# Neighbourhood attention over 160 keys a tile, with the tokens laid out by grid columns

## The reference

```python
h = rmsnorm(x, norm1_g);  proj = h @ w_in + b_in          # width 4352
qa, ka, va, qb, kb, vb, ga, gb = split(proj)
oa = neighborhood_attention(qa, ka, va, rpb)  # 8 heads of 64; a query sees all 4 rows and the 16 grid
                                              # columns nearest to its own (clamped), bias by 2-D offset
ob = sliding_window_gqa(rope(qb), rope(kb), vb, sinks)    # 8 heads, 2 KV heads, |i - j| <= 128
x = x + (sigmoid(ga) * (oa @ w_up_a) + sigmoid(gb) * (ob @ w_up_b)) @ w_out
x = x + moe(rmsnorm(x, norm2_g))              # top 4 of 32 experts: 1024 -> 2 x 1024 -> 1024
return rmsnorm(x, final_g)
```

## Time and profile before

| | |
|---|---|
| median of 3 runs | 1115.62 us |
| lowest and highest | 1115.27 and 1117.86 us |
| the profiled execution | 1115.38 us |
| its span (first to last instruction) | 1113.1 us |
| mean granted clock of TensorE, share of full speed | 0.994 |
| PE busy | 1074.6 us, 97% of the span |
| DVE, ACT, POOL busy | 303.9, 110.8, 43.2 us |
| HBM read | 434.26 MB, 391 GB/s over the span |
| chain that ended last | PE 67%, DMA 26%, SP's queue 4% |

### The profile page before, as it was taken

The page is one execution under the profiler, slowest core; times in us unless marked ns, Lnnn a source line. Parts: engine busy times, 40 slices in busy tenths (PEclk is TensorE's granted clock), DMA queues, the critical chain, the costliest instruction groups (busy, mean ns, idle before and its releaser), DMA issues.

```text
span 1113.1 us, 13392 instructions
## 1 busy us (share of the span) xinstructions
PE 1074.6 (97%) x5309; PEld 479.3 (43%) x5309; DVE 303.9 (27%) x659; ACT 110.8 (10%) x243; POOL 43.2 (4%) x44
## 2 busy tenths in 40 slices
PE   9999999999999999999999999999999999999996
PEld 8888888633333333333333333333332333333332
DVE  4356644222222222122222222222221112222213
ACT  1142520200000000000000000000000000000001
POOL 1106500000000000000000000000000000000000
PEclk9999999999999999999999999999999999999999
DMA  9963379599999999999999999999999999999996
GB/s 360 410 238 121 114 261 389 216 425 427 427 429 429 429 429 427 429 427 427 430 427 429 428 428 429 427 429 427 430 427 430 427 430 427 429 428 429 429 425 277
DMA packets 35641, 435.69 MB, mean 391 GB/s; under 512 B 4384, under 2 KB 4896, under 8 KB 6848
## 3 DMA queue, kind: packets, MB, share of 16 engines
q1 hardware_dynamic: 34608, 434.38, 92.9%
q10 hardware_dynamic: 1008, 0.95, 0.3%
HBM read 434.26 MB, written 1.05 MB: 391 GB/s over the span
## 4 chain that ended last, share of the span: by engine, by line
PE 67%; DMA 26%; SPq 4%; DVE 1%; ACT 1%; issue 0%; POOLq 0%; POOL 0%; DVEq 0%
PE bank L893 26%; DMA ring<-in_w 25%; PE bank L959 13%; PE bank L606 5%; SPq L371 4%; PE bank L854 4%; PE bank L799 4%; PE bank L806 3%; PE bank L708 3%; PE bank L690 2%; PE bank L550 2%; PE bank L602 1%; PE bank L782 1%; PE bank L654 1%; PE bank L627 1%; DMA ring<-in_w_in 1%
## 5 line engine op out<-in xcount | busy, mean ns | idle before, releaser
L893 PE MATMUL bank<-ring,work 128*64 128x512 f32 x2048 | 452.9, 595 | 24.8 <-DMA ring<-in_w 24.8
L893 PEld LDWEIGHTS bank<-ring,work 128*64 128x64 f32 x2048 | 147.1, 137 | 309.6 <-issue 274.9
L959 PE MATMUL bank<-ring,work 128*64 128x512 f32 x1024 | 232.5, 596 | 1.0 <-DVE work L1377 0.6
L1367 DVE TENSOR_SCALAR work<-bank 128x512 f32<-128x512 f32 x32 | 22.1, 692 | 398.3 <-PE bank L893 398.3
L959 PEld LDWEIGHTS bank<-ring,work 128*64 128x64 f32 x1024 | 70.4, 136 | 134.6 <-issue 114.6
L1551 ACT ACTIVATE work<-work 128x512 f32<-128x512 f32 x32 | 20.1, 629 | 696.8 <-DVE work L1367 696.8
L799 PE MATMUL bank<-x2n,work 128*64 128x512 f32 x256 | 68.5, 616 | 0.0
L854 PE MATMUL bank<-work 64*128 64x512 f32 x256 | 63.9, 617 | 0.9 <-DVE work L1345 0.9
L1291 DVE TENSOR_TENSOR work<-bank,vec 128x256 f32<-128x256 f32 (+1 forms) x64 | 24.1, 418 | 144.0 <-PE bank L806 144.0
L806 PEld LDWEIGHTS bank<-cst,work 128*128 128x128 f32 x320 | 33.8, 141 | 54.9 <-DVE work L1374 27.4
L606 PE MATMUL bank<-ring 128*128 128x256 f32 x240 | 54.2, 382 | 0.0
(11 more groups left out here) (203 smaller groups left out, 570.2 us busy)
## 6 DMA issues: line engine op xcount, KB each, us to landing
ring<-in_w SPq DMA_DIRECT2D x184, 2048.0 KB, 36.6
ring<-in_w_in SPq DMA_DIRECT2D x16, 1024.0 KB, 24.1
ring<-in_w SPq DMA_DIRECT2D x15, 1024.0 KB, 12.8
ring<-in_w_out SPq DMA_DIRECT2D x4, 1024.0 KB, 4.9
ring<-in_w_up_a SPq DMA_DIRECT2D x2, 1024.0 KB, 10.8
ring<-in_w_up_b SPq DMA_DIRECT2D x2, 1024.0 KB, 7.3
ring<-in_na_rpb SPq DMA_DIRECT2D x1, 1536.0 KB, 17.2
ring<-in_w SPq DMA_DIRECT2D x2, 512.0 KB, 28.8
```

Source lines behind the costliest of these rows:

```text
L893: last = pe.matmul(bank[CAP * a:CAP * (a + 1), bk, :], kT, pairs[:, pair_of(par, k // 2), at + q * 512:at + (q + 1) * 512], start=False, s ...
L959: last = pe.matmul(bank[CAP * a:CAP * (a + 1), to, :], fT, pairs[:, pair_of(par, c), at + a * 512:at + (a + 1) * 512], start=f == 0, stop= ...
```

## The change

The host hands over the tokens column by column of the grid: token t is now row t % 4, column t // 4. The rotary angles, the sliding window's mask, the neighbourhood mask and the bias table are built for that order on the host, and the host puts the output back in order. A query tile of 128 tokens is then 32 whole grid columns, and the keys that it can see are its own 128 tokens and 32 tokens (8 columns) of the other tile: 160 keys, which are adjacent. For u < 4:

- the 4 score matmuls have 160 columns in place of 256, and bias, maximum, exponentials and division work on 160 keys a tile; the bias is added in one instruction;
- `turn_probs` has 4 transposes of each tile's own 128 keys and 4 matmuls against the identity that put the 32 edge keys of the 4 (head, tile) pairs into the four partition groups of 32, in bank 6; `read_probs` copies 640 elements in place of 1024;
- `attend` has 8 matmuls of 128 columns: for each query tile both heads' own 128 keys, then both heads' 32 edge keys, whose values must lie in the partitions of those keys. `copy_near_values`, new on ACT, puts them there once: 4 copies of 32 x 512, behind the exponentials of unit 0. They go into `biases`, so `b2_sb` is loaded later, behind attention's last transpose. The output lies in banks 6 and 7;
- `turn_probs` of every unit but the first waits for `o_ready` of the unit before;
- `na_bias` shrinks to 1280 KB and the neighbourhood mask grows from 64 to 320 elements a partition (128 KB more of constants).

```diff
@@ -62,7 +61,9 @@
 _W_KEPT = [("ident", P), ("before", P), ("slot", P), ("over", OVER), ("expert", 1), ("groups", PARTS * E), ("fold", E)]
-_W_ATTN = [("cos", T), ("sin", T), ("na_mask", GRID_W),
+NEAR_W = P + 32
+NEAR_AT = T - NEAR_W
...
+def token_places():
+    t = np.arange(T)
+    return t % ROWS, t // ROWS
...
-    ang = np.arange(T, dtype=np.float32)[None, :] * inv[i % half][:, None]
+    row, col = token_places()
+    pos = row * GRID_W + col
+    ang = pos.astype(np.float32)[None, :] * inv[i % half][:, None]
-    col = i % GRID_W
-    first = np.clip(col - NA_COLS // 2, 0, GRID_W - NA_COLS)[:, None]
-    key = np.arange(GRID_W)[None, :]
-    near = np.where((key >= first) & (key < first + NA_COLS), 0.0, NEG)
-    c[:, CONST["na_mask"]] = near
-    q = np.arange(MT)[None, :, None] * P + i[:, None, None]
-    k = np.arange(T)[None, None, :]
-    c[:, CONST["swa_mask"]] = np.where(np.abs(k - q) <= WINDOW, 0.0, NEG).reshape(P, MT * T)
+    first = np.clip(col - NA_COLS // 2, 0, GRID_W - NA_COLS)
+    for m in range(MT):
+        own, key = first[m * P:(m + 1) * P, None], col[None, m * NEAR_AT:m * NEAR_AT + NEAR_W]
+        at = CONST["na_mask"].start + m * NEAR_W
+        c[:, at:at + NEAR_W] = np.where((key >= own) & (key < own + NA_COLS), 0.0, NEG)
+    far = np.abs(pos[None, :] - pos[:, None]) > WINDOW
+    c[:, CONST["swa_mask"]] = np.where(far, NEG, 0.0).reshape(MT, P, T).transpose(1, 0, 2).reshape(P, MT * T)
...
@@ -165,8 +173,8 @@
-        tables = attn_buf(HEADS * DR * GRID_W)
-        na_bias = tables.rearrange("p (h w) -> p h w", h=HEADS)
+        tables = attn_buf(2 * 3 * 4 * P)
+        na_bias = tables[:, 0:HEADS * MT * NEAR_W].rearrange("p (h w) -> p h w", h=HEADS)
+        v_near = biases[:, 0:NA_W]
...
+        def near_T(n):
+            return probT[:].rearrange("p i k t -> p (i k t)")[:, n * P:(n + 1) * P]
@@ -391,11 +404,10 @@
...
-                    sp.dma_start(tables[:], na_rpb).then_inc(bias_landed, 16)
+                    sp.dma_start(tables[:, 0:HEADS * MT * NEAR_W], na_rpb).then_inc(bias_landed, 16)
...
                     sp.dma_start(wr, w_router).then_inc(route_landed, 16)
                     sp.dma_start(br_b[:], bcast(b_router, 0, E)).then_inc(route_landed, 16)
-                    sp.dma_start(b2_sb, b2[0]).then_inc(b2_landed, 16)
 
             up, outp = N_IN, N_IN + N_UP
             load_chunk(1, 0, 1, up - 2)
@@ -403,6 +415,7 @@
             sp.wait_ge(probT_done, UNITS)
             for part in range(PARTS):
                 sp.dma_start(b1_raw[part * E:(part + 1) * E, :], b1[0]).then_inc(b1_landed, 16)
+            sp.dma_start(b2_sb, b2[0]).then_inc(b2_landed, 16)
@@ -478,9 +491,7 @@
...
             for hd in range(HEADS):
-                v = na_bias[:, hd, :].rearrange("p (a c) -> p a c", c=GRID_W)
-                mask = C("na_mask").rearrange("p (o c) -> p o c", o=1).to_broadcast([P, DR, GRID_W])
-                pool.tensor_tensor(v, v, mask, ALU.add).then_inc(masked_bias, 1)
+                pool.tensor_tensor(na_bias[:, hd, :], na_bias[:, hd, :], C("na_mask"), ALU.add).then_inc(masked_bias, 1)
@@ -623,8 +634,11 @@
...
-                        q, k = (qaT, kaT[:, pair, :]) if u < 4 else (qbT[:], kbT[:, pair // 2, :])
-                        last = pe.matmul(bank[:, BS + i, qt * T:(qt + 1) * T], q[rows, pair, qt * P:(qt + 1) * P],
+                        if u < 4:
+                            q, k, width = qaT, kaT[:, pair, qt * NEAR_AT:qt * NEAR_AT + NEAR_W], NEAR_W
+                        else:
+                            q, k, width = qbT, kbT[:, pair // 2, :], T
+                        last = pe.matmul(bank[:, BS + i, qt * width:(qt + 1) * width], q[rows, pair, qt * P:(qt + 1) * P],
                                          k[rows, :], start=True, stop=True)
                 last.then_inc(scores_done, 1)
@@ -634,6 +648,18 @@
                 pe.wait_ge(prob_ready, u + 1)
                 if u:
                     pe.wait_ge(probT_ready, u)
+                    pe.wait_ge(o_ready, u)
+                if u < 4:
+                    for i in range(2):
+                        for qt in range(MT):
+                            own = prob[u % 2][:, i, qt, qt * (NEAR_W - P):qt * (NEAR_W - P) + P]
+                            pe.transpose(quarter(BT)[:, 2 * i + qt, :], own, C("ident"))
+                    for n in range(4):
+                        i, qt = n % 2, n // 2
+                        edge = prob[u % 2][:, i, qt, (1 - qt) * P:(1 - qt) * P + E]
+                        last = pe.matmul(quarter(BT + 1)[E * n:E * (n + 1), 0, :], edge, C("ident"), start=True, stop=True)
+                    last.then_inc(probT_done, 1)
+                    return
                 for i in range(2):
@@ -648,9 +674,21 @@
                 if u:
                     pe.wait_ge(o_ready, u)
+                if u < 4:
+                    pe.wait_ge(v_near_ready, 4)
+                    for qt in range(MT):
+                        dst = [quarter(BT + 1 + qt)[DH * i:DH * i + DH, 2, :] for i in range(2)]
+                        cols = [slice((2 * pair + i) * DH, (2 * pair + i + 1) * DH) for i in range(2)]
+                        for i in range(2):
+                            pe.matmul(dst[i], v_sb[:, qt, cols[i]], near_T(2 * i + qt), start=True, stop=False)
+                        for i in range(2):
+                            rows = slice(DH * qt + E * i, DH * qt + E * (i + 1))
+                            last = pe.matmul(dst[i], v_near[rows, cols[i]], near_T(4)[rows, :], start=False, stop=True)
+                    last.then_inc(o_done, 1)
+                    return
                 for kt in range(2):
                     for i in range(2):
-                        col = (2 * pair + i) * DH if u < 4 else NA_W + pair // 2 * DH
+                        col = NA_W + pair // 2 * DH
                         last = pe.matmul(bank[DH * i:DH * i + DH, BO, 0:T], v_sb[:, kt, col:col + DH],
                                          probT[:, i, kt, :], start=kt == 0, stop=kt == 1)
                 last.then_inc(o_done, 1)
@@ -1139,14 +1178,14 @@
...
-                        bias = na_bias[:, 2 * pair:2 * pair + 2, (2 - 2 * qt) * GRID_W:(2 - 2 * qt + ROWS) * GRID_W]
-                        last = dve.tensor_tensor(s[:, :, qt, :], bank[:, BS:BS + 2, qt * T:(qt + 1) * T], bias, ALU.add)
+                    raw = bank[:, BS:BS + 2, 0:MT * NEAR_W].rearrange("p i (m k) -> p i m k", m=MT)
+                    bias = na_bias[:, 2 * pair:2 * pair + 2, :].rearrange("p i (m k) -> p i m k", m=MT)
+                    last = dve.tensor_tensor(s, raw, bias, ALU.add)
...
-                ch.link(dve.tensor_reduce(mx[:], s[:], AX.X, ALU.max))
+                ch.link(dve.tensor_reduce(mx[:], s, AX.X, ALU.max))
@@ -1164,13 +1203,14 @@
...
                 for i in range(2):
-                    inv = den[:, i, :].rearrange("p (m o) -> p m o", o=1).to_broadcast([P, MT, T])
-                    last = dve.tensor_tensor(s[:, i, :, :], s[:, i, :, :], inv, ALU.mult)
+                    inv = den[:, i, :].rearrange("p (m o) -> p m o", o=1).to_broadcast([P, MT, NEAR_W])
+                    last = dve.tensor_tensor(s[:, i, :, 0:NEAR_W], s[:, i, :, 0:NEAR_W], inv, ALU.mult)
                 last.then_inc(prob_ready, 1)
 
             def read_output(u):
                 dve.wait_ge(o_done, u + 1)
-                dve.tensor_copy(oT[:, u, :], bank[:, BO, 0:T]).then_inc(o_ready, 1)
+                dve.tensor_copy(oT[:, u, :].rearrange("p (m t) -> p m t", m=MT),
+                                bank[:, BT + 1:BO + 1, 2 * P:3 * P]).then_inc(o_ready, 1)
@@ -1448,7 +1488,8 @@
...
-                        last = act.activation(s[:, i, qt, :], s[:, i, qt, :], ACT.Exp,
+                        own = s[:, i, qt, 0:NEAR_W] if u < 4 else s[:, i, qt, :]
+                        last = act.activation(own, own, ACT.Exp,
                                               bias=neg_mx[:, i, qt:qt + 1], accum_out=den[:, i, qt:qt + 1])
@@ -1456,8 +1497,10 @@
...
-                act.activation(probT[:].rearrange("p i k t -> p (i k t)"),
-                               bank[:, BT:BT + 2, :].rearrange("p b n -> p (b n)"), ACT.Identity).then_inc(probT_ready, 1)
+                width = 5 * P if u < 4 else 8 * P
+                act.activation(probT[:].rearrange("p i k t -> p (i k t)")[:, 0:width],
+                               bank[:, BT:BT + 2, :].rearrange("p b n -> p (b n)")[:, 0:width],
+                               ACT.Identity).then_inc(probT_ready, 1)
@@ -1491,10 +1534,19 @@
...
+            def copy_near_values():
+
+                act.wait_ge(proj_read_dve, 6)
+                for n in range(4):
+                    edge = v_sb[0:E, 1, 0:NA_W] if n < 2 else v_sb[P - E:P, 0, 0:NA_W]
+                    act.activation(v_near[n * E:(n + 1) * E, :], edge, ACT.Identity).then_inc(v_near_ready, 1)
+
             for c in range(N_IN):
                 turned, scored = unit_at(TURN_C, c), unit_at(UNIT_C, c)
```

(39 more changed lines are left out.)

## The result

The changed kernel takes 1120.38 us (median of 7 runs, 1119.62 to 1121.53). The kernel before takes 1117.32 us in the runs counted with them (7 runs, 1115.27 to 1118.23). The ratio is 1.0032, with a 95% interval of 1.0023 to 1.0041: slower by 3.06 us, where 1.1 us less was forecast. The profiled execution took 1121.53 us, with a span of 1119.3.

A forecast was written before the change was run, and what follows sets the result against it. TensorE's input projection with attention was taken to set the weight stream's start; 0.33 + 0.04 - 0.09 = 0.28 us less a unit, 1.1 us for four, gave 1114.3, stated as 1114.5 us; range 1112.6 to 1118.0 us.

The forecast's parts named there:

- What bounds the kernel: Experts' stretch: one weight stream of 874.5 us at 428 GB/s, started by TensorE's first expert products, then a 19 us tail.
- The sign that was forecast: Start of the experts: TensorE's first expert product about 1 us earlier, and the weight stream starting as much earlier.
- SP's part: Weight loads behind the moved `b2_sb` load: three pairs issued 0.45 us later, hidden by slack in the transfers, cost nothing.
- POOL's: Masking of the bias table, done at 31.98 us, long ahead of its first reader before 50.39 us.
- Scores: TensorE's score matmuls in a neighbourhood unit: 0.74 us in place of 1.07, 0.33 us less.
- Transposes and edges: TensorE's probability transposes and edge matmuls in a unit: 0.84 us in place of 0.88, 0.04 us less.
- Product with the values: TensorE's 16 records a unit, taken as paired: 1.10 us in place of 1.01, 0.09 us more.
- Rival B: Edge products of two heads take turns on one PSUM bank: product 1.56 us a unit, 1116.2 us total; chance 0.17.
- Rival A: Short TensorE records have a floor, 0.115 us each: unit 1.16 us longer, 1120.0 us total; chance 0.08.
- DVE, ACT, the new waits: Attention units: less DVE and ACT work, ACT's new copies and the new wait in `turn_probs` all costed at nothing.
- a slower stream: Experts' weight stream: pace differing by 0.1% moves the end 0.9 us and hides the gain; rival's chance 0.12.

The follow-up runs named there:

- b_near: Kernel before with 30 never-executed semaphore increments in TensorE's branch that is taken when few tokens are left over; 1117.03 us, ratio 1.0003 to the kernel before.
- b_b2: Kernel before with only the load of `b2_sb` moved behind the three transfers of b1, behind attention; 1116.73 us, ratio 1.0002 to the kernel before.
- a_order: Changed kernel with both tiles' own-key products with the values first, then both tiles' edge-key products; 1118.41 us, ratio 1.0018 to the kernel before.
- a_banks: Changed kernel with a query tile's two heads writing different PSUM banks in the product with the values, copied in two instructions; 1120.00 us, ratio 1.0029 to the kernel before.
- b_far: Kernel before with 100 never-executed semaphore increments in TensorE's branch for experts with more than 64 tokens left over; 1119.33 us, ratio 1.0029 to the kernel before.
- a_pad: Changed kernel with 64 executed TensorE semaphore increments, 16 ahead of each of chunks 2, 3, 4 and 10; 1119.30 us, ratio 1.0024 to the kernel before.
- a_mid: Changed kernel with the product with the values ordered own keys tile 0, edges tile 1, edges tile 0, own keys tile 1; 1121.16 us, ratio 1.0036 to the kernel before.
- b_early: Kernel before with 96 executed TensorE semaphore increments, 32 ahead of each of chunks 2, 3 and 4; 1122.86 us, ratio 1.0055 to the kernel before.

## Why the prediction was wrong

- **What bounds the kernel** held. The stream starts with TensorE's first expert products and takes 890.6 us against 889.6, within the scatter that b_near shows, at 428 GB/s. The sign that was forecast didn't come: these products start at 215.63 us, where they started at 213.23. SP's part is hidden (b_b2), and TensorE doesn't wait for POOL's.
- **Scores**: 0.74 forecast, 0.75 measured.
- **Transposes and edges**: 0.84 forecast, 0.89 measured, and 0.10 more in the products behind them, which the sum didn't have.
- **Product with the values**, the step that failed in attention: 1.10 forecast, 1.47 measured. I took pairing for granted across all 16 records, by rows of groups in which all records have one tile shape. The order written in the change goes from 128 x 64 to 32 x 64 and back, and each such change costs. With the groups joined (a_order) the step takes 0.96 us, and attention as a whole is 1.0 us shorter: the 1.1 us of the forecast. Rival B gave nearly the right figure (1.56) for a wrong reason, as a_banks shows. Rival A's floor isn't there either: 0.047 us a record in the joined edges.
- **DVE, ACT, the new waits**: no term, and none measured. ACT's four copies (in the last fence, below) took 2.58 us and ended at 54.92 us, 0.6 us later than the exponentials of unit 1 would otherwise have begun, with the first reader at 60.34. The one wait of TensorE for another engine between chunks 1 and 16, 0.7 us for ACT's copy of unit 4, was there before.
- **The tail** wasn't in the sum at all: 2.84 us in the profile, and 1.65 to 3.09 us in the other kernels with the pause. No term or rival of mine ended there. I counted the 48 records as work and not as code. The Trainium skill (Runtime: NRT & Kernel Launch, section Instruction fetch mechanics) says that code comes in blocks of 16 KB, and that a taken branch whose target isn't at hand has to wait for its fetch. b_far's trace agrees: its branch lasts 3.86 us, with 16 KB of code on the queue meanwhile. In the changed kernel the branch was no slower than before and its first instruction was at hand; the wait came right behind it, with 2.6 us from the packet's start to the next product. That the engine waited for this packet is inferred from the order in time and from the runs that moved the code; no view names it.

Together: 1.0 us of attention and 1.65 to 3.09 us of tail make 2.6 to 4.1 us, and 3.06 us were measured. The stated 1114.5 us is 5.9 us too low: 3.06 us of loss, 1.1 us of gain that didn't come, and 1.7 us by which the median of seven runs of the kernel before, 1117.32 us, lies above that of the first three. So the upper end of my range, 1118.0 us, which was to leave room for B and a slower stream, lay 0.7 us above the kernel before, and left none for a cause that I hadn't listed.

Open: how many blocks the engine holds, and when it fetches one ahead. The distance from the branch to its target alone doesn't decide. It is 293 instructions in the kernel before and in the changed one alike (places 4673 to 4966 and 4769 to 5062, by what b_near and b_late expected), and a_pad, another 64 further on, has no pause. b_far's target, at 5066, misses; the changed kernel's, at 5062, is at hand, and the code right behind it isn't. That fits one boundary of blocks between 5062 and 5066. In a_pad a piece of code was fetched at 1103.2 us, 3 us ahead of the branch, while the changed kernel's last one ahead of its branch came at 1081.7 us; so a_pad seems to have crossed a boundary early enough to have the next block at hand. Open too is why the clock was lowered behind the pause in the changed kernel, a_order, a_mid and b_early, and not in b_far and a_banks; pauses of 2.9 and of 3.6 us are among the latter. And whether kernels built on the changed one have a stream longer by some tenths of a microsecond is below what these runs tell.

ACT in order of time, changed kernel:

```profile
52.34 2.58 ACT L1542 ACTIVATE biases<-ring 32x512 f32<-32x512 f32 x4 [4.03 <-DVE ring L1094]
54.94 0.43 ACT L1492 ACTIVATE ring<-ring,neg_mx 128x160 f32<-128x160 f32 x1
```

## What to carry to other kernels

A tile product cut down to fewer keys can get slower, as here, when it falls into alternating groups of two tile shapes: group calls of one tile shape, and count every change of shape (0.15 to 0.35 us here) in the sum. When a change lengthens an engine's program ahead of a branch over seldom used code, look at the last block behind that branch for idle time put down to "issue"; padding of the same length in the old kernel tells code from work. And compare single profiles by stages, not by spans: the start and the stream alone moved by 1 to 2 us between executions of the same code.

## What the runs showed of the hardware

- 100 instructions never executed, between a branch and its target, cost 2.8 us (the branch itself lasted 3.86 us in place of 0.35); 30 cost nothing that the runs tell (b_far, b_near).
- With the same distance from branch to target, but 96 instructions further on, the branch took 0.35 us and the second instruction behind it came 3.1 us after the first (after).
- Semaphore increments of TensorE cost 0.065 us each where they are not hidden (1.04 us for 16, a_pad). Sixteen ahead of each of three chunks of products vanished; 32 cost 4.2 us in three chunks (b_early).
- Eight float32 records of 32 x 64 weights at four places of the array and 128 columns take 0.38 us, and four of them in a group 0.37 us (a_order, after).
